# Two weight slots taken together behind each layer norm, in one Trainium2 kernel

## The reference

```python
for l in range(DEPTH):                                    # DEPTH = 2
    mod = jax.nn.silu(c) @ w_ada[l] + b_ada[l]
    sh1, sc1, g1, sh2, sc2, g2 = jnp.split(mod[:, None, :], 6, axis=-1)
    h = x * (1.0 + sc1) + sh1
    y = token_mixer(h, ...)                               # h @ w_in[l], two attentions, w_out[l]
    x = layer_norm(DEEPNORM_ALPHA * x + g1 * y, ln1_g[l], ln1_b[l])
    h = x * (1.0 + sc2) + sh2
    y = conv_ffn(h, ...)                                  # h @ w_up[l], 3-tap conv, silu gate, w_down[l]
    x = layer_norm(DEEPNORM_ALPHA * x + g2 * y, ln2_g[l], ln2_b[l])
return x
```

## Time and profile before

| | |
|---|---|
| median of three runs | 2331.97 us |
| the profiled execution | 2331.93 us, of which 2330.1 us are the span from first to last instruction |
| PE busy | 2292.8 us, 98% of the span, 11342 matmuls |
| DVE, ACT, POOL busy | 1261.0, 1001.2, 996.8 us |
| mean granted TensorE clock | 0.998 of full speed |
| DMA | 249.47 MB read from HBM, 110 GB/s over the span |

### The profile page before, as it was taken

One profiled execution on the slowest core, in us unless ns is written; L12 is line 12 of the kernel. 1 busy time (PEld: TensorE's weight loads), 2 busy tenths in 40 slices (PEclk: granted clock), 3 DMA queues, 4 the chain that ended last, 5 costly groups with the idle time before them and its releaser, 6 DMA issues.

```text
span 2330.1 us, 32114 instructions
## 1 busy us (share of the span) xinstructions
PE 2292.8 (98%) x11342; PEld 1860.4 (80%) x11342; DVE 1261.0 (54%) x2669; ACT 1001.2 (43%) x1673; POOL 996.8 (43%) x894
## 2 busy tenths in 40 slices
PE   7999999999999999999999999999999999999998
PEld 4888878888888888887888888888888877788767
DVE  8765766844435378468486344315630163186684
ACT  7454455344433254544534343423142354333473
POOL 3432223544444453313245444445554434455472
PEclk9999999999999999999999999999999999999999
DMA  9641143332226354313442322223222321222211
GB/s 348 242 141 61 64 129 142 119 101 97 90 80 246 108 193 152 100 42 104 137 171 73 104 94 90 87 99 116 96 90 90 108 77 37 90 91 91 91 46 37
DMA packets 52646, 260.62 MB, mean 112 GB/s; under 512 B 6640, under 2 KB 16368, under 8 KB 26928
## 3 DMA queue, kind: packets, MB, share of 16 engines
q1 hardware_dynamic: 51376, 250.68, 31.2%
q0 software_dynamic: 1152, 8.39, 0.9%
HBM read 249.47 MB, written 7.34 MB: 110 GB/s over the span
## 4 chain that ended last, share of the span: by engine, by line
PE 81%; issue 10%; POOL 4%; DVE 2%; ACT 1%; DMA 1%; SPq 0%; POOLq 0%; DVEq 0%; ACTq 0%
PE bank L762 23%; PE bank L764 22%; PE bank L763 22%; POOL w_lo L615 4%; PE bank L1017 3%; PE bank L925 1%; PE bank L1022 1%; PE bank L1281 1%; PE bank L914 1%; PE bank L900 1%; DMA ada_early<-w_ada 1%; PE bank L1270 1%; PE bank L1435 1%; PE bank L877 0%; PE bank L1454 0%
## 5 line engine op out<-in xcount | busy, mean ns | idle before, releaser
L615 POOL TENSOR_TENSOR w_lo<-w_raw,w_hi 128x512 fp32r<-128x512 f32 (+2 forms) x732 | 878.2, 1231 | 1152.8 <-ACT w_hi L1487 767.7
L762 PE MATMUL bank<-h_hi,w_hi 128*128 128x512 f32 x1616 | 644.2, 399 | 0.7 <-POOL w_lo L615 0.7
L764 PE MATMUL bank<-h_hi,w_lo 128*128 128x512 f32 x1616 | 630.5, 390 | 0.0
L763 PE MATMUL bank<-h_lo,w_hi 128*128 128x512 f32 x1616 | 629.4, 389 | 0.0
L764 PEld LDWEIGHTS bank<-h_hi,w_lo 128*128 128x128 f32 x1616 | 303.3, 188 | 64.7
L762 PEld LDWEIGHTS bank<-h_hi,w_hi 128*128 128x128 f32 x1616 | 304.0, 188 | 61.5 <-issue 2.4
L763 PEld LDWEIGHTS bank<-h_lo,w_hi 128*128 128x128 f32 x1616 | 304.0, 188 | 58.7 <-issue 1.0
L1487 ACT ACTIVATE w_hi<-w_raw 128x2048 fp32r<-128x2048 f32 (+2 forms) x108 | 189.9, 1758 | 274.5 <-PE bank L764 253.6
L2404 DVE SCALAR_TENSOR_TENSOR cv<-bank,par,cv 128x511 f32<-128x511 f32 (+1 forms) x176 | 131.7, 749 | 213.5 <-ACT cv L1758 200.6
L1492 ACT ACTIVATE w_hi<-w_raw 128x2048 fp32r<-128x2048 f32 x68 | 129.9, 1910 | 125.5 <-PE bank L764 117.0
L1758 ACT ACTIVATE cv<-bank,par 128x512 f32<-128x512 f32 x88 | 68.3, 779 | 233.7 <-PE bank L764 232.0
(11 more groups left out here) (384 smaller groups left out, 3836.5 us busy)
## 6 DMA issues: line engine op xcount, KB each, us to landing
w_raw<-w_stream SPq DMA_DIRECT2D x150, 1024.0 KB, 4.9
w_raw<-w_down SPq DMA_DIRECT2D x32, 704.0 KB, 4.0
ada_mid<-w_ada SPq DMA_DIRECT2D x20, 1024.0 KB, 5.7
ada_last<-w_ada SPq DMA_DIRECT2D x12, 1024.0 KB, 4.9
ada_early<-w_ada POOLq DMA_DIRECT2D x8, 1024.0 KB, 15.9
ada_late<-w_ada SPq DMA_DIRECT2D x8, 1024.0 KB, 6.5
bias_in<-bias_scratch SPq DMA_DIRECT2D x16, 256.0 KB, 3.1
bias_in<-bias_scratch SPq DMA_DIRECT2D x16, 192.0 KB, 2.7
```

Of the source, the lines that this page charges most:

```text
L615: ins = nc.gpsimd.tensor_tensor(w_lo[r][:, part], w_raw[r][:, part], w_hi[r][:, part].bitcast(fp32), ALU.subtract)
L762: nc.tensor.matmul(out, w[0][:, cols], xh, start=first, stop=False)
L763: nc.tensor.matmul(out, w[0][:, cols], xl, start=False, stop=False)
L764: return nc.tensor.matmul(out, w[1][:, cols], xh, start=False, stop=last)
```

## The change

Behind all four norms the first two slots are taken together (`first_slots`, called with the norm's number). PE gives each of the first five chunks to four tiles, in banks 0 to 3, then finishes the tiles one after the other with the last three chunks. The chunks of the norm now go through banks 4 and 5. The second slot is split in four pieces of 512 columns inside the norm: pieces 0 and 2 (the first four chunks of its two tiles) by ACT ahead of the square root and by POOL ahead of its subtractions, piece 1 by ACT behind the root, piece 3 behind the first chunk, and 1 and 3 by POOL after two of its six subtractions. Waits for new semaphores `w_piece` and `w_part` order the pieces.

Three more edits go with it: the two loads of positions count on `loaded`, the load of the last gain counts on `tab_loaded`, and a chain in the rotation of q uses the engine's own chain semaphore.

```diff
+            def lo_piece(n, part):
+                at = slice(512 * part, 512 * part + 512)
+                return nc.gpsimd.tensor_tensor(w_lo[n % 2][:, at], w_raw[n % 2][:, at], w_hi[n % 2][:, at].bitcast(fp32),
+                                               ALU.subtract)
...
-            def norm_sub(l, which):
+            def norm_sub(l, which, n):
                 k = 2 * l + which
+                pool.wait_ge(w_piece, k + 1)
+                lo_piece(n, 0)
+                lo_piece(n, 2).then_inc(w_part, 1)
                 pool.wait_ge(rest_ready, k + 1)
                 pool.wait_ge(var_ready, k + 1)
                 for f in range(2, KD):
+                    if f == 4:
+                        pool.wait_ge(w_hi_done, n + 1)
+                        lo_piece(n, 1)
+                        lo_piece(n, 3).then_inc(w_ready, 1)
...
+            def first_slots(l, m, t, number):
+                ws = (split(l, m), split(l, m + 1))
+                base = KD * (number + 1)
+                wait_slot(l, m)
+                for q in range(4):
+                    wait_bank(l, t + q)
...
+                for k in range(5):
+                    pe.wait_ge(h_hid, base + k + 1)
+                    for q in range(4):
+                        if k == 0 and q == 2:
+                            pe.wait_ge(var_ready, number + 1)
+                            pe.wait_ge(w_part, number + 1)
+                        if k == 4 and q == 2:
+                            wait_slot(l, m + 1)
+                        high(q, k)
+                    if k:
+                        pe.wait_ge(h_ready, base + k)
+                        for q in range(4):
+                            low(q, k - 1)
+                for q in range(4):
+                    for k in range(5, KD):
+                        if q == 0:
+                            pe.wait_ge(h_hid, base + k + 1)
+                        high(q, k)
+                        if q == 0:
+                            pe.wait_ge(h_ready, base + k)
+                        low(q, k - 1)
+                    if q == 0:
+                        pe.wait_ge(h_ready, base + KD)
+                    low(q, KD - 1).then_inc(tile_done, 1)
...
-                first_slot(l, SLOT_UP, TILE_UP, h_hi, h_lo, h_hid, KD * hidx(l, 1), h_ready, KD * hidx(l, 1))
-                slot_tiles(l, SLOT_UP + 1, TILE_UP + 2)
+                first_slots(l, SLOT_UP, TILE_UP, 2 * l)
...
+                act.wait_ge(w_full[n % 2], 16 * (n // 2 + 1))
+                piece(0)
+                piece(2).then_inc(w_piece, 1)
                 act.wait_ge(var_ready, k + 1)
                 A_(ln_tok[:, 4:8], ln_tok[:, 4:8], ACT.Sqrt, bias=ln_eps).then_inc(std_done, 1)
+                piece(1)
                 act.wait_ge(centred, k + 1)
                 A_(ht[0][:, :], banks[5][:, :], ACT.Copy).then_inc(rest_ready, 1)
...
-                    A_(h_hi[:, j, :], banks[2 + j % 2][:, :], ACT.Identity, bias=ln_gb[:, 8 + j:9 + j]).then_inc(h_hid, 1)
-                    if j < 4:
-                        part = slice(512 * j, 512 * j + 512)
-                        ins = A_(w_hi[n % 2][:, part], w_raw[n % 2][:, part], ACT.Copy)
-                        if j == 3:
-                            ins.then_inc(w_hi_done, 1)
+                    A_(h_hi[:, j, :], banks[4 + j % 2][:, :], ACT.Identity, bias=ln_gb[:, 8 + j:9 + j]).then_inc(h_hid, 1)
+                    if j == 0:
+                        piece(3).then_inc(w_hi_done, 1)
```

More of the change, by code:

```diff
@@ L272, in build @@
         w_half = sem("w_half")
+        w_piece = sem("w_piece")
+        w_part = sem("w_part")
         lo_helped = sem("lo_helped")
@@ L331, in build @@
         q_turn = sem("q_turn")
-        q_cross_done = sem("q_cross_done")
         q_stored = sem("q_stored")
@@ L464, in score @@
             return banks[4 + min(b, 2)][:, at:at + S - b * P]
-        LOADS = 16 * 3
+        LOADS = 16 * 5
         BIAS_UNITS = [(i, 8 * i + q) for i in range(NB) for q in range(8)]
@@ L474, in _ @@
         def _(sp):
-            sp.dma_start(posi[:, :], a["pos"]).then_inc(pos_loaded, 16)
-            sp.dma_start(qposi[:, :], a["qpos"]).then_inc(pos_loaded, 16)
+            sp.dma_start(posi[:, :], a["pos"]).then_inc(loaded, 16)
+            sp.dma_start(qposi[:, :], a["qpos"]).then_inc(loaded, 16)
             sp.dma_start(selc[:, :], a["consts"][:, C_SEL:NC]).then_inc(loaded, 16)
@@ L664, in _ @@
                 lo(n + SLOT_UP)
-                norm_sub(l, 0)
-                lo(n + SLOT_UP + 1)
+                norm_sub(l, 0, n + SLOT_UP + 1)
                 lo_loop(n + SLOT_UP + 2, SLOT_DOWN - SLOT_UP - 2, SLOT)
@@ L669, in _ @@
                 lo(n + SLOTS)
-                norm_sub(l, 1)
-                lo(n + SLOTS + 1)
+                norm_sub(l, 1, n + SLOTS + 1)
             def token_factor(number):
@@ L1025, in first_slot, with high, low @@
                                 ins.then_inc(tile_done, 1)
+            def first_slots(l, m, t, number):
[4 more added lines that the diff above has]
+                    wait_bank(l, t + q)
+                def high(q, k):
+                    cols = slice(q % 2 * D + k * P, q % 2 * D + (k + 1) * P)
+                    for part in range(2):
+                        nc.tensor.matmul(banks[q][:, :], ws[q // 2][part][:, cols], h_hi[:, k, :],
+                                         start=(k == 0 and part == 0), stop=False)
+                def low(q, k):
+                    return nc.tensor.matmul(banks[q][:, :], ws[q // 2][0][:, q % 2 * D + k * P:q % 2 * D + (k + 1) * P],
+                                            h_lo[:, k, :], start=False, stop=(k == KD - 1))
+                for k in range(5):
[22 more added lines that the diff above has]
+                    low(q, KD - 1).then_inc(tile_done, 1)
@@ L1027, in _ @@
             for l in range(DEPTH):
-                first_slot(l, SLOT_IDX, TILE_IDX, h_hi, h_lo, h_hid, KD * hidx(l, 0), h_ready, KD * hidx(l, 0))
+                if l:
+                    first_slots(l, SLOT_IDX, TILE_IDX, 2 * l - 1)
+                else:
+                    first_slot(l, SLOT_IDX, TILE_IDX, h_hi, h_lo, h_hid, KD * hidx(l, 0), h_ready, KD * hidx(l, 0))
                 for m in range(1, 4):
@@ L1031, in _ @@
                         pe.wait_ge(bias_out, 8 * NB)
-                    slot_tiles(l, SLOT_IDX + m, TILE_IDX + 2 * m)
+                    if l == 0 or m > 1:
+                        slot_tiles(l, SLOT_IDX + m, TILE_IDX + 2 * m)
                     if m == 2:
@@ L1216, in turned_tiles @@
             def turned_tiles(m, t, slots, which):
-                first_slot(2, m, t, h_hi, h_lo, h_hid, KD * hidx(2, which), h_ready, KD * hidx(2, which))
-                slot_tiles(2, m + 1, t + 2)
+                if which:
+                    first_slot(2, m, t, h_hi, h_lo, h_hid, KD * hidx(2, which), h_ready, KD * hidx(2, which))
+                    slot_tiles(2, m + 1, t + 2)
+                else:
+                    first_slots(2, m, t, 2 * DEPTH - 1)
                 tiles_loop(2, m + 2, t + 4, slots - 2)
@@ L1613, in norm_tail, with piece @@
                 k = 2 * l + which
+                n = slot_no(l, split_after)
+                def piece(part):
+                    at = slice(512 * part, 512 * part + 512)
+                    return A_(w_hi[n % 2][:, at], w_raw[n % 2][:, at], ACT.Copy)
+                act.wait_ge(w_full[n % 2], 16 * (n // 2 + 1))
+                piece(0)
+                piece(2).then_inc(w_piece, 1)
                 act.wait_ge(var_ready, k + 1)
                 A_(ln_tok[:, 4:8], ln_tok[:, 4:8], ACT.Sqrt, bias=ln_eps).then_inc(std_done, 1)
+                piece(1)
                 act.wait_ge(centred, k + 1)
@@ L2243, in norm_tail @@
                         dve.wait_ge(h_hid, KD * (k + 1) + j + 1)
-                        V.scalar_tensor_tensor(h_lo[:, j, :], banks[2 + j % 2][:, :], ln_gb[:, 8 + j:9 + j], f32(h_hi[:, j, :]),
+                        V.scalar_tensor_tensor(h_lo[:, j, :], banks[4 + j % 2][:, :], ln_gb[:, 8 + j:9 + j], f32(h_hi[:, j, :]),
                                                ALU.add, ALU.subtract).then_inc(h_ready, 1)
@@ L2329, in _ @@
                 dve.wait_ge(q_turn, 2 * l + 1)
-                V.tensor_tensor(q_back[:, :], first, rope[:, S:2 * S], ALU.mult).then_inc(q_cross_done, 1)
-                dve.wait_ge(q_cross_done, 5 * l + 1)
-                V.tensor_tensor(first, first, rope[:, 0:S], ALU.mult).then_inc(q_cross_done, 1)
+                chain(V.tensor_tensor(q_back[:, :], first, rope[:, S:2 * S], ALU.mult))
+                V.tensor_tensor(first, first, rope[:, 0:S], ALU.mult)
                 dve.wait_ge(q_turn, 2 * l + 2)
-                V.tensor_tensor(q_cross[:, :], second, rope[:, S:2 * S], ALU.mult).then_inc(q_cross_done, 1)
-                dve.wait_ge(q_cross_done, 5 * l + 3)
+                chain(V.tensor_tensor(q_cross[:, :], second, rope[:, S:2 * S], ALU.mult))
```

(5 more changed lines are left out.)

10 lines of the change are left out of this document (2 added, 8 removed).

## The result

| kernel | median, us | lowest to highest | runs |
|---|---|---|---|
| before, on the same chip | 2332.74 | 2331.8 to 2333.51 | 4 |
| changed | 2351.45 | 2349.99 to 2353.09 | 4 |

The changed kernel is slower: ratio 1.0081, interval 1.0069 to 1.0093. The direction was forecast; the time, 2343.9 us, is some 7.5 us short, and 2351.45 lies above the range's upper end of 2349.5. The profiled execution took 2351.77 us, 19.84 more than that of before.

The account below looks back on a forecast made before the run. PE, busy 98% of the span, was taken as the bound. To the profiled 2331.93 us came 10.3 for late third slots (4.1 of removed gaps already included) and 1.7 for the clock: 2343.9 us, range 2338.0 to 2349.5.

Parts of the forecast that it names:

- What bounds the kernel: Whole kernel: PE is busy 98% of the span, so any lateness of PE adds to the time one for one.
- Gaps removed, nothing in the norm's chain: First two slots: PE's waits for chunks go, 4.1 us over norms one, two and four; pieces in the norm cost nothing.
- The third slot: Behind each norm: buffers released later, PE stalls, third slot late by 2.0, 2.6, 3.4, 2.3 us, 10.3 with gaps included.
- The clock: Behind the four stalls: half clock after one of four, at 1.72 us, so +1.7 us.
- The upper bound: Clock behind the four stalls: at most 4 x 1.72 = 6.9 us.
- the half clock at 46 us: Start of the kernel: the 9.2 us wait was read as followed by a clock of 0.50, agreeing with the cited rule.
- The rival with the half clock behind each stall: Third slots: all four stalls bring slow matmuls, 10.3 + 6.9 = 17.2 us, 2349.1 us; chance 0.23 for more than two falls.
- PE did not stay dense: Rival at the third slots: PE stays dense, only the 4.1 us of gaps count, 2327.8 us; chance 0.05.
- no delay was taken up: Rival after the third slots: a later wait not driven by PE absorbs part of 10.3 us, 2336 or less; chance 0.05.
- The lengthened chain: Rival inside the norms: pieces delay the root by some 0.3 us each, 1.2 us more, 2345.1 us; chance 0.05.

Follow-up runs that it names:

- e6_long: Changed kernel with all eight chunks given to the four tiles in turn, so the first slot's buffers come free 18 matmuls later: 2369.66 us, ratio 1.0155 to before.
- e5_fill7: Changed kernel with seven unneeded matmuls behind each pair of slots, filling part of PE's stall: 2348.08 us, ratio 1.0068 to before.
- e4_one: Changed kernel with only three chunks of one second-slot tile beside the first slot, POOL doing one piece before its subtractions, three behind: 2330.31 us; again 2331.07.
- e2_split_only: Changed kernel with PE back to one slot after the other, the second slot's pieces still split inside the norm: 2337.89 us, ratio 1.0021 to before.
- e1_fill: Changed kernel with 14 unneeded matmuls behind each of the four pairs of slots, filling PE's stall: 2343.29 us, ratio 1.0045 to before.
- e7_one_late: e4_one with POOL released for its early piece behind ACT's second piece instead of its first: 2330.09 us, ratio 0.9987 to before.

## Why the prediction was wrong

**What bounds the kernel: right.** Every lateness of PE went into the end: 19.75 us by the landmarks, 19.84 us of time.

**Gaps removed, nothing in the norm's chain: right.** The landmark waits 0.43 us for `ln_tok` in both kernels, and PE ran dry 481.11 - 3.46 - 453.17 = 24.48 us behind it, against 2.46 + 21.76 = 24.22 plus what a last matmul lasts longer than its spacing (0.16), which leaves 0.1. ACT still idled 0.51 us ahead of the root, where the forecast left 0.3, as its timeline shows beside the earlier trace rows:

```profile
450.96 1.13 ACT L1675 ACTIVATE w_hi<-w_raw 128x512 fp32r<-128x512 f32 x2
452.61 0.30 ACT L1681 ACTIVATE ln_tok<-ln_tok,ck 128x4 f32<-128x4 f32 x1 [0.51 <-DVE ln_tok L2284]
...
473.30 0.78 ACT L1820 ACTIVATE cv<-bank,par 128x512 f32<-128x512 f32 x1 [1.42 <-PE bank L1050]
473.98 1.91 ACT L1549 ACTIVATE w_hi<-w_raw 128x2048 fp32r<-128x2048 f32 x1
```

The scaling of chunk 4 waited 1.21 us for POOL, as computed at 1.2, against the earlier trace rows. This is DVE's timeline:

```profile
460.95 0.75 DVE L2300 SCALAR_TENSOR_TENSOR bank<-x,ln_gb,bank 128x512 f32<-128x512 f32 x1 [1.21 <-POOL x L647]
```

**The third slot: right.** Stalls of 3.4, 3.9, 3.4 and 3.7 were forecast, 3.46, 3.77, 3.44 and 3.65 came. The delays were 2.37, 2.63, 1.93 and 2.50 against 2.0, 2.6, 3.4 and 2.3. The third differs because before's fall at 1240 us did not recur; with its 1.72 us the delay is 3.65. Without that fall's effect the sum is 11.15 us, forecast 10.3.

**The clock: the step that failed.** "I take the share of the nearest rows, one of four: +1.7." All four stalls were followed by the half clock, and three of the four cost 2.6 to 3.0 us, not 1.72: 10.1 us in place of 1.7. Other falls moved by 1.7 - 1.46 - 1.72 = -1.5 us, so the clock's net share is 8.6; 11.15 + 8.6 gives the 19.75.

Both factors were wrong. The frequency came from stretches of thin work, in which PE still issues narrow matmuls; behind stalls of this length, in which PE stands still, the fall came each time. The upper bound took the one price that the trace showed, 1.72, as the largest one; by e6_long even a stall of 8 us costs 1.7 to 3.1, so four of them at about 3 would have been the bound to keep, but no row of the kernel before had that price.

A reading was wrong as well. The prediction puts the half clock at 46 us behind the 9.2-us wait at the start. That wait ends at 9.22 us, and the windows of the kernel before show a clock of 1.00 from there to 44 us, as in the two below. What its timeline of PE has just ahead of the fall is narrow matmuls with a wait of 1.80 us between them. So these rows show no half clock behind a stall of 3 us or more, and the start can't be said to agree with the rule that the prediction cites. PE's first two groups of eight matmuls of L834, at 14.64 and 16.99 us, do take 1.94 and 1.37 us where later ones take 1.03 to 1.07; why, no run settles.

```profile
20.00:22.00 2.00, 2.00 (x37) 1.52 (x32) 1.48 (x5) 1.78 (x5) 0.00 (x0) 1.00 1.01 422
42.00:44.00 2.00, 0.83 (x12) 0.27 (x12) 2.00 (x6) 2.00 (x4) 0.00 (x0) 1.00 1.10 381
...
43.13 0.83 PE L824 MATMUL bank<-step,wb 128*32 128x512 bf16 x12 [1.80 <-DVE step L1982]
```

The rival with the half clock behind each stall had the mechanism and gave 2349.1; with 10.1 in place of its 6.9 us it would have given 2352.3, beside 2351.77 of the profiled execution. That it comes so close is in part luck: delays 0.85 us longer than forecast and other falls 1.5 us fewer partly cancel. The rule that the prediction cited, the Trainium skill, "TensorE: Matmul & The Clock Gate", section "HAM oscillation", that waiting gaps bring the half clock back and cost again each time, agrees here with four stalls of four in the changed kernel; of e5_fill7's shorter ones, one of four brought none.

**The other rivals.** PE did not stay dense and no delay was taken up. The lengthened chain was absent in the changed kernel. In e4_one, where the root did come late, it cost 0.57 us at each norm, 2.3 us in all and not the 1.2 of the rival; the late chunk 4 of e2_split_only cost 3.8 us.

## What to carry to other kernels

When work is reordered so that a stall goes, look at when the buffers come free: here the interleaving that won 4.1 us of gaps moved the release 28 matmuls later, and the third slots came 11 us late in all, the gain included; interleaving only as much as fills the gaps was the version that won, by some 2 us of 2332. A stall of an otherwise dense TensorE is to be counted with the half clock behind it: here it came each time behind 3.4 to 8.9 us, and three times of four behind some 2 us. Where the trace at hand has no stall of that length, rows in which PE worked thinly do not give its frequency or its price, and the range has to hold a fall behind each stall at more than the one price seen. Where a stall of some microseconds can't be avoided, matmuls nobody needs, put into it, can pay for themselves: here 8.2 us, though the kernel stayed slower than before.

## What the runs showed of the hardware

- The stretch behind a stall ahead of the third slot grew by 1.6 to 3.0 us behind 3.4 to 3.8 us of idle PE (changed kernel) and by 1.7 to 3.1 behind 7.8 to 8.9 (e6_long), so no more behind the longer stall. Behind 1.9 to 2.2 us (e5_fill7) the half clock came three times of four, at 1.7 us, behind 0.3 to 0.7 (e1_fill) never.
- A square of 128x4 on DVE (L2281), both inputs in SBUF, took 0.85 us when a subtraction of POOL had begun 0.44 us before it (e4_one), and 0.16 us when it began first (e7_one_late). The Trainium skill, "SBUF — State Buffer", section "Who interferes with whom", says that a VectorE instruction with two SBUF inputs is held up by a GpSimd instruction that reads SBUF and started earlier; the two runs agree.
